# Three raw and five split weight buffers in place of eight and seven

## The reference, cut to what matters

```
# block 1
z    = rmsnorm(x);  proj = z @ w_in                       # 2048 -> 3072
y    = concat(pool_mixer(proj[:1024]), rg_lru(proj[1024:2048]) * gelu(proj[2048:]))
h    = x + y @ w_out
q    = rmsnorm(h) @ peer_wq                               # 8 heads, product keys
top16 of 128 + 128 keys -> top16 of 16384 experts per head and token, softmax gate
h    = h + sum_k gate_k * gelu(u_k . z) * v_k;  x = rmsnorm(h)
# block 2
proj = rmsnorm(x) @ w_in_2 + b_in_2                       # q, k, v, glu_a, glu_b, gate_sb, gate_cv
o_sb = stick_breaking_attention(q, k, v) @ w_sb_out       # 8 heads of 128
u    = silu(layernorm(causal_depthwise_conv31(glu_a * sigmoid(glu_b))));  o_cv = u @ w_conv_out
x    = x + rmsnorm((sigmoid(gate_sb) * o_sb + sigmoid(gate_cv) * o_cv) @ w_o)
x    = x + rmsnorm(relu(rmsnorm(x) @ w_up)**2 @ w_down)
```

## Time and profile before

| | |
|---|---|
| median of 3 runs | 3356.66 us |
| profiled execution, its own time | 3359.69 us |
| its span (first to last instruction) | 3357.9 us |
| mean granted TensorE clock | 0.981 |
| PE busy | 3210.6 us, 96% of the span |
| DVE, POOL, ACT busy | 2311.1, 2086.7, 1676.4 us |
| moved by DMA | 615.45 MB, 183 GB/s on average |

### The profile page before, as it was taken

How to read it: one execution, slowest core, us unless ns; L and a number is a source line. 1 busy time by engine, 2 the same in 40 slices (tenths; PEclk the granted TensorE clock), 3 DMA queues, 4 the chain that set the end, 5 groups by cost and what they waited for, 6 DMA issues and landing times.

```text
span 3357.9 us, 48527 instructions
## 1 busy us (share of the span) xinstructions
PE 3210.6 (96%) x18206; PEld 2791.0 (83%) x18206; DVE 2311.1 (69%) x2875; ACT 1676.4 (50%) x2618; POOL 2086.7 (62%) x1890
## 2 busy tenths in 40 slices
PE   7999989999999999999999998899998899999997
PEld 6788878888888888888888877788887788888886
DVE  8756898855666666665657679899654856666564
ACT  5554446644545444454545645455656444444443
POOL 3677777864756666575747866556776444444456
PEclk9999999999999999999999999999999999999999
DMA  6455545666666656565665554445555455555553
GB/s 215 150 190 166 178 157 189 206 208 206 189 213 191 211 188 208 187 210 186 202 194 187 188 174 145 140 155 188 189 176 163 149 187 186 188 186 186 187 188 126
DMA packets 177720, 615.45 MB, mean 183 GB/s; under 512 B 18129, under 2 KB 34897, under 8 KB 176081
## 3 DMA queue, kind: packets, MB, share of 16 engines
q1 hardware_dynamic: 157824, 572.59, 53.4%
q10 hardware_dynamic: 19664, 39.76, 3.3%
HBM read 593.41 MB, written 18.87 MB: 182 GB/s over the span
## 4 chain that ended last, share of the span: by engine, by line
PE 71%; DVE 15%; POOL 7%; ACT 4%; issue 3%; DMA 0%; ACTq 0%; POOLq 0%; DVEq 0%
PE G L407 47%; PE G L408 24%; DVE lo L1001 4%; DVE CV L1297 3%; POOL lo L1476 3%; ACT hi L636 2%; DVE oneB L1276 2%; POOL tS L1481 1%; DVE tS L1007 1%; POOL tS L1536 1%; DVE oneA L1278 0%; ACT oneB L810 0%; POOL tS L1538 0%; DVE ZA L1320 0%; POOL oneB L1631 0%
## 5 line engine op out<-in xcount | busy, mean ns | idle before, releaser
L407 PE MATMUL G<-ZA,hi 128*128 128x512 f32 x5120 | 1830.0, 401 | 42.4 <-DVE lo L1001 12.4
L1001 DVE TENSOR_TENSOR lo<-raw,hi 128x768 fp32r<-128x768 f32 (+3 forms) x1088 | 1380.9, 1286 | 327.5 <-ACT hi L636 326.7
L1476 POOL TENSOR_TENSOR lo<-raw,hi 128x256 fp32r<-128x256 f32 (+2 forms) x1082 | 1326.7, 1235 | 400.4 <-ACT hi L636 399.6
L408 PE MATMUL G<-ZA,lo 128*128 128x256 f32 x5120 | 1441.0, 281 | 0.0
L407 PE MATMUL G<-ZB,hi 128*128 128x512 f32 x3584 | 1263.9, 398 | 11.3 <-DVE ZB L1285 6.5
L407 PEld LDWEIGHTS G<-ZA,hi 128*128 128x128 f32 x5120 | 972.3, 190 | 278.4 <-DVE lo L1001 17.7
L636 ACT ACTIVATE hi<-raw 128x1024 fp32r<-128x1024 f32 x1088 | 1105.9, 1051 | 40.6 <-DMA raw<-in_pv 29.5
L408 PE MATMUL G<-ZB,lo 128*128 128x256 f32 x3584 | 1004.2, 280 | 0.0
L408 PEld LDWEIGHTS G<-ZA,lo 128*128 128x128 f32 x5120 | 976.6, 191 | 0.5
L407 PEld LDWEIGHTS G<-ZB,hi 128*128 128x128 f32 x3584 | 674.9, 188 | 177.9 <-issue 4.5
L408 PEld LDWEIGHTS G<-ZB,lo 128*128 128x128 f32 x3584 | 677.9, 189 | 0.0
(11 more groups left out here) (264 smaller groups left out, 1569.4 us busy)
## 6 DMA issues: line engine op xcount, KB each, us to landing
raw<-in_pu SPq DMA_DIRECT2D x256, 512.0 KB, 3.6
raw<-in_pv SPq DMA_DIRECT2D x256, 512.0 KB, 3.6
raw<-in_w_in SPq DMA_DIRECT2D x192, 512.0 KB, 3.5
raw<-in_w_up SPq DMA_DIRECT2D x128, 512.0 KB, 3.5
raw<-in_w_down SPq DMA_DIRECT2D x128, 512.0 KB, 3.5
raw<-in_w_out SPq DMA_DIRECT2D x32, 512.0 KB, 3.5
raw<-in_wq SPq DMA_DIRECT2D x32, 512.0 KB, 3.5
g_scratch<-stage ACTq DMA_DIRECT2D x16, 1024.0 KB, 4.8
```

The costliest lines, as they stand in the source:

```text
L407: pe.matmul(G[:, 0:512], hi[h % NW][:, k % 8, :], Z[:, k, :], start=first, stop=False, skip_group_check=True)
L408: m = pe.matmul(G[:, 0:256], lo[h % NRAW][:, k % 8, :], Z[:, k, 0:256], start=False, stop=last, skip_group_check=True)
L1001: dve.tensor_tensor(lo[r][:, 0:c, :], raw[r][:, 0:128 * c].rearrange("p (k n) -> p k n", k=c), hi[w][:, 0:c, :].bitcast(F32), ALU.subtract ...
L1476: pool.tensor_tensor(lo[r][:, c:8, :], raw[r][:, 128 * c:1024].rearrange("p (k n) -> p k n", k=8 - c), hi[w][:, c:8, :].bitcast(F32), ALU. ...
```

## The change

The pair of tile rings is changed. `raw` gets 3 buffers and `lo` 5 buffers of its own, `hi` goes from 7 to 5. SP's wait changes with it: the DMA of half h waits until DVE and POOL have made `lo` of half h-3 (`s_lo`, and `s_lop` where POOL had a part), no longer until PE has finished half h-8. The splits of walk u are for the halves 2u+3 and 2u+4, where they were for 2u+5 and 2u+6; in walk 0 two are made and not four. The two splits placed by hand before unit 416 move by two halves in the same way. The region `rr` grows to 39 KB, some of its layouts are put together otherwise, UC0 to UC4 no longer lie over SGC, and ACT's wait at SGC's tile 10 goes. The number of matmuls, splits, evacuations and DMAs is the same.

```
-NRAW = 8
-NW = 7
+NRAW = 3
+NW = 5
 def pool_part(h):
-    if h == 2 * M0 + 5:
+    if h == 2 * M0 + 3:
         return 7
 def split_ahead(u):
-    return [h for h in ((3, 4, 5, 6) if u == 0 else (2 * u + 5, 2 * u + 6)) if h < NH]
+    return [h for h in (2 * u + 3, 2 * u + 4) if h < NH]
...
-        wts = [region(4096, f"wts{i}", [(f"raw{i}", ...)], [(f"lo{i}", ...)]) for i in range(NRAW)]
-        raw, lo = [wts[i][f"raw{i}"] for i in range(NRAW)], [wts[i][f"lo{i}"] for i in range(NRAW)]
+        raw = [sb(f"raw{i}", [128, HALF]) for i in range(NRAW)]
         hi = [sb(f"hi{i}", [128, 8, 128], F32R) for i in range(NW)]
+        lo = [sb(f"lo{i}", [128, 8, 128], F32R) for i in range(NW)]
...
-        rr = region(32768, "rr_mem",
+        rr = region(39 * 1024, "rr_mem",
...
-                    [("SGS", [128, 16, T], F32), ("SGC", [128, 16, T], F32)],
-                    [("rr_pad6", [128, 6752], F32),
+                    [("SGS", [128, 16, T], F32), ("SGC", [128, 16, T], F32),
                      ("UC0", [128, 288], F32), ("UC1", [128, 288], F32), ("UC2", [128, 288], F32),
...
         def sync_program(sp_):
             for h, (u, p) in enumerate(HALVES):
                 if h >= NRAW:
-                    sp_.wait_ge(s_mm, h - NRAW + 1)
+                    sp_.wait_ge(s_lo, h - NRAW + 1)
+                    if POOL_SPLITS[h - NRAW]:
+                        sp_.wait_ge(s_lop, POOL_SPLITS[h - NRAW])
                 sp_.dma_start(raw[h % NRAW][:, :], weights(u, p)[0]).then_inc(s_raw[h % NRAW], 16)
...
                 if st == "sg" and part == 3:
-                    if c and i == 10:
-                        act.wait_ge(s_dw, 8 * TAPS)
...
             def prep(h):
-                dve.tensor_tensor(lo[r][:, 0:c, :], raw[r][:, 0:128 * c]..., hi[w][:, 0:c, :]..., ALU.subtract)
+                dve.tensor_tensor(lo[w][:, 0:c, :], raw[r][:, 0:128 * c]..., hi[w][:, 0:c, :]..., ALU.subtract)
```

More of the change, by code:

```diff
@@ L183, in region @@
             return out
-        wts = [region(4096, f"wts{i}", [(f"raw{i}", [128, HALF], F32)], [(f"lo{i}", [128, 8, 128], F32R)]) for i in range(NRAW)]
-        raw, lo = [wts[i][f"raw{i}"] for i in range(NRAW)], [wts[i][f"lo{i}"] for i in range(NRAW)]
+        raw = [sb(f"raw{i}", [128, HALF]) for i in range(NRAW)]
         hi = [sb(f"hi{i}", [128, 8, 128], F32R) for i in range(NW)]
+        lo = [sb(f"lo{i}", [128, 8, 128], F32R) for i in range(NW)]
         ZA = sb("ZA", [128, 16, 512], F32R)
@@ L215, in build @@
                      ("mr0", [128, 256], F32), ("mr1", [128, 256], F32)],
[L216 removed]
                     [("eq1", [128, 8, 16, 16], F32), ("rr_pad5", [128, 8, T], F32), ("eq0", [128, 8, 16, 16], F32)],
[L218 to L219 removed]
+                    [("rr_pad2", [128, 16, T], F32), ("rr_pad3", [128, 16, T], F32),
+                     ("cd0", [128, 2, 64], F32), ("cd1", [128, 2, 64], F32), ("dg", [128, 4, 256], F32),
+                     ("tpf", [128, 2, 128], F32), ("sm", [128, 4, 16], F32)],
                     [("rr_pad4", [128, 24, T], F32), ("oneB0", [128, 8, 128], F32), ("oneB1", [128, 8, 128], F32)],
                     [("U1", [128, 16, T], F32), ("U2", [128, 16, T], F32)],
[L222 to L223 removed]
+                    [("SGS", [128, 16, T], F32), ("SGC", [128, 16, T], F32),
                      ("UC0", [128, 288], F32), ("UC1", [128, 288], F32), ("UC2", [128, 288], F32),
@@ L404, in product @@
             def product(u, p, n, k, G, first, last):
-                h = POS[u][p]
+                w = POS[u][p] % NW
                 Z = weights(u, p)[1]
-                pe.matmul(G[:, 0:512], hi[h % NW][:, k % 8, :], Z[:, k, :], start=first, stop=False, skip_group_check=True)
-                m = pe.matmul(G[:, 0:256], lo[h % NRAW][:, k % 8, :], Z[:, k, 0:256], start=False, stop=last, skip_group_check=True)
+                pe.matmul(G[:, 0:512], hi[w][:, k % 8, :], Z[:, k, :], start=first, stop=False, skip_group_check=True)
+                m = pe.matmul(G[:, 0:256], lo[w][:, k % 8, :], Z[:, k, 0:256], start=False, stop=last, skip_group_check=True)
                 if n == 7:
@@ L649, in evac @@
                     if u == M0 - 1:
-                        prep(2 * M0 + 5)
+                        prep(2 * M0 + 3)
                     low(u)
@@ L762, in post_mix @@
                     if n == 6:
-                        prep(2 * M0 + 6)
+                        prep(2 * M0 + 4)
             def gate_split(c, part):
@@ L1000, in prep @@
                 dve.wait_ge(s_hi, h + 1)
-                dve.tensor_tensor(lo[r][:, 0:c, :], raw[r][:, 0:128 * c].rearrange("p (k n) -> p k n", k=c),
+                dve.tensor_tensor(lo[w][:, 0:c, :], raw[r][:, 0:128 * c].rearrange("p (k n) -> p k n", k=c),
                                   hi[w][:, 0:c, :].bitcast(F32), ALU.subtract).then_inc(s_lo, 1)
@@ L1475, in prep @@
                     pool.wait_ge(s_hi, h + 1)
-                    pool.tensor_tensor(lo[r][:, c:8, :], raw[r][:, 128 * c:1024].rearrange("p (k n) -> p k n", k=8 - c),
+                    pool.tensor_tensor(lo[w][:, c:8, :], raw[r][:, 128 * c:1024].rearrange("p (k n) -> p k n", k=8 - c),
                                        hi[w][:, c:8, :].bitcast(F32), ALU.subtract).then_inc(s_lop, 1)
```

2 lines of the change are left out of this document (1 added, 1 removed).

## The result

The changed kernel takes 3384.41 us (median of 4 runs, 3382.20 to 3389.79) against 3357.45 (also 4 runs) for the kernel before, 27.0 us more. Over all timed executions, 21 of the changed kernel with a median of 3385.79, the ratio is 1.0092, 95% interval [1.0078, 1.0107], or 31 us. Its profiled execution took 3385.48 us with a span of 3383.7.

A forecast was written before the change was run, and what follows sets the result against it. The prediction took PE's matmuls as the bound. Start -3, routing +12, convolution +10 and lead +8 sum to +27 us on 3356.7, giving 3384 us, with bounds of 3366 to 3408 us and an 8-in-10 range of 3358 to 3418.

The forecast's parts named there:

- The kernel is bound by PE, a change of buffers acts at its stops: Whole kernel: PE is busy 96% of the span, so buffers can cost or give only at PE's stops.
- Start, -3: Start: two splits fewer before the second sum of squares and fewer bytes ahead of x, -3 us (-4 to 0).
- Routing, +12: Routing: raw ring shortages delay DVE and PE waits for the one-hot matrices, +12 us (4 to 20).
- the ring's shortage: Routing and convolution: DVE stands still where under 4.6 us separate a walk's first split from the next walk's second.
- Quiet walks, nothing: Some 430 of 544 walks: the margin falls from 11.0 to 5.4 us, so the shorter lead costs nothing.
- Convolution, +10: Convolution: 23 walks short by 16 us together, 10 after halving, nothing takes them up, +10 us (4 to 18).
- the halving: Routing and convolution: of two shortages in a row, half of the second is counted; the convolution's 16 us become 10.
- hidden-shortage rival: All stages: DVE's standing is repaid by shorter instructions, ring costs 4 not 22 us, 3366 us; chance 0.13.
- Lead, +8: After the last attention stop: splits come 5.6 us nearer to use; 5.0 us stall plus 3, +8 us (5 to 13).
- Nothing else behind the last attention step: Behind the last attention step: only the lead was given a cost; ring shortages were counted up to 2287 us.
- The waits for `oneA` and `sp` keep their sum: Sign in the profile: PE's `oneA` and `sp` waits keep about their sum, `lo` waits grow 15 us or more.
- PE's pace: Rival, whole kernel: if both slower stretches ran at the quick pace, 31 us less, 3353 us; chance 0.09.

The follow-up runs named there:

- e1: Kernel before, its buffers kept, with splits three halves ahead as in the changed kernel (the lead alone): 3353.61 us, ratio 1.0002.
- e12: Kernel of e1, with SP also waiting for the split three halves back for halves 84 to 189 alone, the routing: ratio 1.0031.
- e4: Kernel of e3 with five raw tiles in place of three: 3359.66 us, ratio 1.0013.
- e3: Changed kernel with the 32 KB `rr` region and ACT's wait of before put back: 3385.48 us, ratio 1.0096.
- e2: Kernel before, its buffers and five halves of lead kept, with SP also waiting for the split three halves back: 3391.00 us, ratio 1.0106.
- e8: Kernel of e3 with four raw tiles in place of three: 3361.23 us, ratio 1.0024.
- e5: Kernel of e1 with e2's wait for halves 640 to 723 alone, the convolution: ratio 1.0016.
- e6: Kernel of e1 with e2's wait for halves 724 to 769 alone, the gates and layer norm: ratio 1.0031.
- e7: Kernel before, with three halves of lead before walk 20, four splits in that walk and five halves of lead from there: 3358.76 us, ratio 1.0013.
- e9: Kernel before, with three halves of lead before walk 200, four splits in that walk and five halves of lead from there: 3352.87 us, ratio 1.0004.
- e10: Kernel of e3 with two raw tiles: 3871.07 us in one run.

## Why the prediction was right, step by step

The total was right: 27 us forecast, 25.8 by the span, 27.0 by the medians and 31 by the ratio. The terms were not all right. The forecast had -3 for the start, +12 for the routing, +10 for the convolution and +8 for what follows it; the stops came as -3, +13, +4 and +18. That one term too high and one missing cost nearly cancel is luck.

*The kernel is bound by PE, a change of buffers acts at its stops.* Right: of the 25.8 us of the span 19.7 are standing time, and PE's busy time grew by 6.1 (3210.6 to 3216.7).

*Start, -3.* Right: stops -3.0 up to unit 20, of which the lead alone gives 2.1 (e1). The second sum of squares begins at 33.70 before, at 31.66 in e1 and at 30.86 after. The rest goes with fewer bytes ahead of x: ACT's wait for its second piece was 1.30 us before, 1.02 in e1 and 0.30 after.

*Routing, +12.* Right in size (+13.0 in units 56 to 88; +12.5 and 10 us for the wait alone, e12), and the mechanism is there (4.54 us from release to split). But the stretch is made up of two parts, only one of which was foreseen, so the size is partly luck. From unit 56 to 80 the shift grows by 8.8 us: that is the forecast's own mechanism, for which it had 12. The other 4.3 come between units 80 and 88 (e4, without the ring's shortage, has 3.9 there between 84 and 88), and not from a split that a late transfer held up: ACT sends the gates to DRAM and back, and the write has become slower. The page's issues of before and after:

```profile
g_scratch<-stage ACTq DMA_DIRECT2D x16, 1024.0 KB, 4.8
```
```profile
g_scratch<-stage ACTq DMA_DIRECT2D x16, 1024.0 KB, 7.6
```

In the last such exchange e4 issues the write at 639.01 and the read at 650.18, 11.2 us later; in e1 it is 641.23 and 647.73, 6.5 us. ACT stands behind the read with the next copies. In all kernels of the table in which the routing's transfers follow the splits (after, e3, e12, e2, also e4 and e8, with five and four tiles) the page has 7.4 to 7.6 us for the write, in the others (e1, e5, e6, e7, e9) 4.8. That weight transfers fall on the write is likely from this, but no run moved them alone.

*Quiet walks, nothing.* Right: units 88 to 312 have -0.6 us of stops, and two raw tiles (e10) show how near the limit is.

*Convolution, +10.* Too high: 3.2 us more shift at unit 356 than at 312, +2.7 of stops with the wait alone. The shortages were there (10.0 us of idle time in e5, 15.1 in the changed kernel, for 10 after and 16 before the halving); the step that failed is "here nothing takes them up". The relief of the hidden-shortage rival does: more than half comes back in shorter DVE instructions. This rival was given only as a whole, for all stages; in the routing it isn't enough (DVE's mean split falls there from 1.31 to 1.17 us, and the stretch still has its 13 us of stops).

*Lead, +8.* Right: +5.9 in stops and +6.9 in the shift between units 356 and 384 when it is changed alone (e1).

*Nothing else behind the last attention step.* Wrong: the shift from unit 356 to 384 is 19.1 us (15.6 in the second trace), 7 of the lead and 9 to 12 of the ring. I had counted the ring's shortages against the trace of before, walk by walk, up to 2287 us. But a shortage depends on when the splits before it ended, and with three halves of lead and DVE late these are late too; the margin that is to be won back after each long piece is what the ring takes. The +10 of the convolution came as 3, and this cost of 9 to 12 had not been forecast at all: ring in both 12 to 15 against 10, near only by luck.

*The waits for `oneA` and `sp` keep their sum.* Wrong for `sp`: 23.7 to 13.9. The prediction's own argument (a stall ahead of it makes the stop shorter) says so; the sentence on the signs forgot it. The waits for `lo` grew by 41 us (44.1 + 12.5 against 2.7 + 12.4), 10 of which came out of `sp`.

*PE's pace.* The two paces are real, but 173.3 and 176.9 ns are 3.5 apart and not 4.4, so the rival was worth 25 us and not 31 (7067 matmuls). For the lead's sum, in which a half counted as 2.76 us, the difference is 0.3 us. What one sees of it: 592 halves went at the slower pace in the trace of the kernel before, 494 in the changed kernel's and 363 in its second, the last two 7.3 us apart for the same program. Halves with a stop are in none of these counts. It is no effect of the change over the long stretches. It needs many executions to average out, and one pair of profiles can be off by 7 us by it alone.

## What to carry to other kernels

A ring of buffers costs nothing as long as its round (release, issue, landing, use) fits in the time its tiles last. Work it out from rows, here 4.6 us between two splits; here one tile too few was the larger part of 0.9%, and one more took three quarters of it back. Look for the cost not in the mean walk but behind the long instructions of the engine that releases the tiles: they delay the next transfer, and it delays that engine again. A stall ahead of a stop that another engine ends is free; behind the last such stop it is paid. When one engine's stall lets another finish work that slows the first, a part of it comes back. To compare two profiles of such a kernel, count stops and pace apart, take a second trace of the same program to see what repeats, and don't take a total that fits for a sum of terms that do.

## What the runs showed of the hardware that was not expected

- PE's clock after a stop. PE's stop of 3.29 us at unit 378 was followed by 5.4 us at a granted clock of 0.50, the lower level (1.2 GHz), where a matmul of 512 columns took 0.63 and not 0.40 us:

```profile
2400.10:2405.50 5.40, 5.40 (x17) 4.62 (x18) 3.22 (x4) 3.50 (x6) 4.41 (x4) 0.50 0.67 206
2405.50:2412.00 6.50, 6.50 (x38) 5.64 (x37) 2.72 (x4) 3.44 (x6) 4.14 (x4) 0.99 0.64 227
```

The half that began there lasted 5.26 us where 2.83 is usual around it, so the stop cost 3.3 + 2.4 us. This is most of why the shift at unit 380 is 6.2 us larger than at unit 378, and why a stop's own length is not its price. In the kernel before, the same place has no such stop.

- The landing of 512 KB rose from 3.5 to 3.9 us in the changed kernel, where SP issues in pairs behind the splits, and was 3.5 to 3.6 again with two tiles. It goes with the distance between two issues: in the changed kernel a transfer issued 1 to 2 us behind the one before took 4.3 to 4.5 us (290 transfers, medians), one issued 2.5 us or more behind it 3.5 to 3.6 (590); in the kernel before 974 of the 1088 were issued 2.5 to 3 us apart and took 3.5. By the fit of the Trainium skill (SBUF — State Buffer, "The DMA setup-cost knee"), 2 us plus the bytes by 436 GB/s, one would estimate 3.2 us; the rows have 3.5 to 3.9, and the measurement decides.
- The same DVE instruction of the convolution takes 0.48 us with POOL idle beside it and 0.90 with POOL at work. So DVE's standing gave back 8.3 us of 15.1 there.
- The same program runs PE at 173.3 or 176.9 ns for a matmul at full granted clock (1.00), for hundreds of us at a time; what chooses is open.
